# One copy moved behind three others in the experts' loop, and a sum put ahead of a maximum in the attention

## What is computed

```python
def block(args):  # differential attention, per block of 128 queries
    s = jnp.einsum('bhcqd,bhcsd->bhcqs', q_blk, kt).astype(f32) * scale
    p = jax.nn.softmax(jnp.where(mask, s, -jnp.inf), axis=-1)
    attn = p[:, :, 0] - lam * p[:, :, 1]
    return jnp.einsum('bhqs,bhsd->bhqd', attn.astype(v.dtype), vt)

def expert_block(args):  # one expert, on the tokens that chose it
    xb, e = args
    hid = jax.nn.silu(xb @ w_gate[e]) * (xb @ w_up[e])
    return hid @ w_down[e]
```

## Time and profile before

| what | value |
|---|---|
| median of 3 runs | 1429.94 us (1427.81 to 1430.13) |
| the profiled execution, its time | 1428.23 us |
| its span, first to last instruction | 1426.5 us |
| TensorE matmuls busy | 1378.9 us, 97% |
| weight loads busy | 1081.4 us, 76% |
| VectorE busy | 997.4 us, 70% |
| ScalarE busy | 793.3 us, 56% |
| mean granted clock of TensorE | 0.986 |
| the experts | about 350 to 865 us |
| the differential attention | about 122 to 215 us |

### The profile page before, as it was taken

How to read it: one execution, slowest core, us unless ns; L and a number is a source line. 1 busy time by engine, 2 the same in 40 slices (tenths; PEclk the granted TensorE clock), 3 DMA queues, 4 the chain that set the end, 5 groups by cost and what they waited for, 6 DMA issues and landing times.

```text
span 1426.5 us, 20296 instructions
## 1 busy us (share of the span) xinstructions
PE 1378.9 (97%) x6801; PEld 1081.4 (76%) x6802; DVE 997.4 (70%) x1209; ACT 793.3 (56%) x984; POOL 197.5 (14%) x234
## 2 busy tenths in 40 slices
PE   6999999998999999999999989999999999999998
PEld 6887778785777777777777767766888888888886
DVE  7866465657999999999989888675845314343185
ACT  5444457225899999999889882543234212332121
POOL 2021002001232222222222120061000000000000
PEclk8999999999999999999999999999999999999999
DMA  9111115156999999999999976002313313224221
GB/s 353 62 60 59 59 35 177 75 186 265 400 413 408 413 413 413 413 412 412 402 405 410 405 260 255 29 32 92 116 59 119 114 64 118 92 86 162 71 107 59
DMA packets 60967, 302.57 MB, mean 212 GB/s; under 512 B 9700, under 2 KB 11810, under 8 KB 48108
## 3 DMA queue, kind: packets, MB, share of 16 engines
q1 hardware_dynamic: 49420, 282.15, 50.3%
q10 hardware_dynamic: 6288, 11.44, 2.4%
q0 software_dynamic: 5200, 8.18, 1.7%
HBM read 291.74 MB, written 18.87 MB: 218 GB/s over the span
## 4 chain that ended last, share of the span: by engine, by line
PE 74%; DMA 4%; DVE 4%; issue 2%; ACT 2%; POOL 0%; DVEq 0%; SPq 0%; ACTq 0%; POOLq 0%
PE ps L784 14%; PE ps L1066 12%; PE ps L1051 11%; PE ps L823 7%; PE ps L816 4%; PE ps L632 3%; PE ps L793 3%; PE ps L1100 3%; PE ps L884 3%; DMA ring<-in_w_gate 3%; PE ps L956 2%; PE ps L544 2%; PE ps L495 1%; DMA ring<-in_w_in 1%; PE ps L773 1%
## 5 line engine op out<-in xcount | busy, mean ns | idle before, releaser
L2245 DVE TENSOR_TENSOR ring_r<-ring,hi 128x2048 fp32r<-128x2048 f32 (+1 forms) x224 | 431.4, 1980 | 20.3 <-ACT hi L1631 18.9
L1631 ACT ACTIVATE hi<-ring 128x2048 fp32r<-128x2048 f32 (+1 forms) x224 | 362.7, 1661 | 8.5 <-DMA ring<-in_w_gate 7.2
L2259 DVE TENSOR_TENSOR ring_r<-ring,ring_two 128x2048 fp32r<-128x2048 f32 (+1 forms) x50 | 103.8, 2107 | 112.2 <-ACT ring_two L1649 112.2
L1649 ACT ACTIVATE ring_two<-ring 128x2048 fp32r<-128x2048 f32 (+1 forms) x46 | 84.0, 1868 | 132.4 <-PE ps L1066 121.5
L784 PE MATMUL ps<-ring_r,XTS 128*128 128x512 f32 x512 | 129.2, 395 | 5.1 <-DVE ring_r L2245 3.1
L1273 POOL TENSOR_TENSOR rsv<-msv,half 128x1 f32<-128x1 f32 (+2 forms) x32 | 33.0, 1035 | 686.1 <-DVE msv L1818 671.4
L784 PE MATMUL ps<-hi,XTS 128*128 128x512 f32 x512 | 127.4, 391 | 0.0
L1066 PE MATMUL ps<-ring_two,ats 128*128 128x512 f32 x512 | 126.5, 389 | 0.0
L823 PE MATMUL ps<-hi,HIDS 128*64 128x512 f32 x512 | 123.5, 393 | 0.0
L784 PEld LDWEIGHTS ps<-ring_r,XTS 128*128 128x128 f32 x512 | 97.3, 190 | 28.1 <-issue 5.6
L544 PE MATMUL ps<-ring_r,ring_r 128*128 128x512 f32 x448 | 116.4, 409 | 1.0 <-ACT ring_r L1426 0.7
(11 more groups left out here) (366 smaller groups left out, 2219.8 us busy)
## 6 DMA issues: line engine op xcount, KB each, us to landing
ring<-in_w_gate SPq DMA_DIRECT2D x32, 2048.0 KB, 15.8
ring<-in_w_down SPq DMA_DIRECT2D x32, 2048.0 KB, 16.0
ring<-in_w_up SPq DMA_DIRECT2D x32, 2048.0 KB, 17.5
ring<-in_w_ff SPq DMA_DIRECT2D x16, 2048.0 KB, 7.9
ring<-in_w_in SPq DMA_DIRECT2D x9, 2048.0 KB, 9.2
ring<-in_w_out SPq DMA_DIRECT2D x4, 2048.0 KB, 10.6
results<-M SPq DMA_DIRECT2D x4, 1024.0 KB, 16.6
ring<-results SPq DMA_DIRECT2D x8, 512.0 KB, 7.6
```

Source lines behind the costliest of these rows:

```text
L1631: act.activation(HI[u][:, c], ring[:, s, c], ACT.Copy).then_inc(w_hi, 1)
L1649: act.activation(hi_of(u, a, part_size(u)), raw_of(u, a, part_size(u)), ACT.Copy).then_inc(w2_hi, 1)
L2245: vec.tensor_tensor(ring_r[s][:, c], ring[:, s, c], HI[u][:, c].bitcast(F32), ALU.subtract).then_inc(w_lo, 1)
L2259: ins = vec.tensor_tensor(raw_of(u, a, n, ring_r), raw_of(u, a, n), hi_of(u, a, n).bitcast(F32), ALU.subtract)
```

## The change

Three edits. On VectorE, `mixed(n - 1)` moves from behind the maximum, `final_d` and `mean_final` to the head of step n. On ScalarE, the keys of block 3 are copied at step 7, no longer at step 5 (those of block 2 stay at step 3). In the experts, high part 1 of the next gate unit moves from between the silu (L1667) and the gated rows' high parts (L1674) to behind these and the next rows' high part (L1635). Nothing is added or removed, and the count of each semaphore stays.

```diff
@@ scalar, the attention's steps
-                if n in (3, 5):
-                    keys_again(TT - 2 + n // 2 - 1)
+                if n in (3, 7):
+                    keys_again(TT - 2 + n // 4)
@@ scalar, block_act
                 act.activation(SG, ps[:, 2, 0:FT * BLK].rearrange("p (f b) -> p f b", f=FT),
                                ACT.Silu).then_inc(sg_ready, 1)
-                if ahead:
-                    weights_hi(e + 1, 1, 1 - odd)
                 for pair in range(2):
                     act.wait_ge(hid_gated, g * 2 + (pair + 1))
...
                 rows_hi(g + 1)
                 if ahead:
-                    for part in range(2, 5):
+                    for part in range(1, 5):
                         weights_hi(e + 1, part, 1 - odd)
@@ vector, the attention's steps
             for n in range(len(ITEMS) + 2):
+                if 1 <= n <= N_D:
+                    mixed(n - 1)
                 if n < N_D:
                     maximum(n)
...
-                if 1 <= n <= N_D:
-                    mixed(n - 1)
```

## The result

| what | before | after |
|---|---|---|
| median (lowest to highest of 5 runs) | 1429.94 us (1427.81 to 1430.76) | 1439.0 us (1434.23 to 1444.45) |
| ratio to before, 95% interval | | 1.0075, 1.0053 to 1.0097 |
| the profiled execution: time, span | 1428.23, 1426.5 us | 1439.0, 1437.3 us |
| TensorE matmuls busy | 1378.9 us, 97% | 1382.1 us, 96% |
| mean granted clock of TensorE | 0.986 | 0.984 |

The kernel is slower by 0.75% by the ratio of the runs; the two medians differ by 9.1 us, 0.63%. H is still the start of the gated rows' high parts; its line is L1672 in the changed kernel, and the other lines behind the edits moved by one or two as well. The experts lose 15.0 us, the attention gives 6.7 back.

A forecast was written before the change was run, and what follows sets the result against it. The prediction took a loop through ScalarE's copies and VectorE's low parts, 15.56 us per expert, to set the pace. Profiled 1428.2 + 13 (experts) + 8 (clock) - 5 (mixer) = 1444 us, range 1434 to 1454.

The forecast's parts named there:

- The loop: Experts, through ScalarE's copies and VectorE's low parts: copy 1 adds 0.97, 0.24 returns, period 15.56 to 16.29 us; stage +13.
- Idle time before H: Experts, ScalarE: a sign of being right was about 0.8 us idle before the gated rows' high parts.
- TensorE's wait at L816: Experts: TensorE would wait 0.19 + 0.73 = 0.92 us for the gated rows' high part in each expert.
- The clock: Experts: longer TensorE waits let its clock drop, 0 to 30 times at about 0.8 us; 10 drops taken, 8 us.
- Rival C: Experts: the clock falls in nearly every expert, 24 us instead of 8, total 1460; chance 0.10.
- The stream: Experts' weights: no longer binds at period 16.29; gate units land in 9 to 12 us to the end.
- rival B: Experts: the weights' stream sets the stage's end, so 4 to 5 of the 13 us remain, total 1427; chance 0.06.
- The last two periods: End of the experts: the period after expert 29 is set by TensorE and stays; the last is 0.7 us longer.
- The attention: Mixer: the sum ahead of the maximum removes 3.2 us of TensorE waits and a 1.7 us clock loss; -5, bounds 0 and -7.
- Rival D: Mixer: no gain because another wait takes over; total 1449, with few drops 1441; chance 0.10.
- The keys' move: Attention, key copies going from step 5 to 7: nothing either way, 0.5 us at most.
- Rival A: Experts: ScalarE's 1.16 us idle absorbs the copy, period stays 15.56, only the mixer's 5 us show, total 1423; chance 0.08.

The follow-up runs named there:

- the third place: Kernel before with only high part 1 of the next gate unit moved, to ahead of the up result's copy: 1427.9 us, period 15.56.
- the kernel with copy 5 first: High part 5 copied ahead of the two result copies: in the changed kernel 1433.99 us, period 16.06; in the kernel with the attention's edits alone 1426.14 us, period 15.86.
- the filled wait: Changed kernel plus matmuls with unused results ahead of TensorE's wait for the gated rows' high part: seven took 1454.83 us, three 1436.0 us.
- the lighter stream: Only half of each down unit loaded, one run each: on the kernel before 1413.59 us, on the changed kernel 1433.95 us.
- the swap alone: Kernel before with only VectorE's sum (`mixed`) moved ahead of the maximum, keys still copied at step 5: 1425.78 us, one run.

## Why the prediction was right, point by point

The forecast was 1444 (1434 to 1454), slower at 0.87; 1439.0 was measured. The mechanism of the experts' part is the one forecast. That the total is 5 us off and not more is partly luck: the stage lost 6 us less than forecast and the attention gained 1.7 more, while 2.4 us that the forecast left at nothing came in elsewhere.

- **The loop.** Forecast 16.29, measured 16.22. Its pieces, in the order of the forecast: 0.89, 5.50 for four copies (forecast 0.97 + 4.56), 0.95 for the result copies, 1.96, 6.61, 0.31. So the loop from row to row was the right one; 0.07 off, 2 us over the stage. Copy 1's old place was worth nothing, as said, and the third place shows that an empty place costs nothing. That low parts 3 and 4 "end just before copy 5 does" holds within 0.17 us; VectorE's side of the loop is as long as 16.06, as the kernel with copy 5 first shows.
- **Idle time before H.** Forecast 0.8, measured 1.56. From the silu to H it was 608.69 to 609.96, 1.27 us, filled by silu and copy 1; now it is 619.34 to 621.28, 1.94, that is 0.67 more, and only the silu's 0.39 is in it. The forecast counted the growth and left out the place of the copy itself. This time is not on the path.
- **TensorE's wait at L816**: 0.92 forecast, 0.87 measured.
- **The clock.** Forecast 10 falls at 0.8, 8 us; measured 6 at 0.92, 5.5 us (three in the experts' edit alone, with the same wait). The number of falls was the mis-sized term. The count could be bounded only, and the price was right. Rival C gave a fall in nearly every expert. The Trainium skill, "TensorE: Matmul & The Clock Gate", section "A second HAM failure mode: psum-queue depth-cycling", has frequent tiny pauses make the clock swing between its levels; the mechanism is borne out by the filled wait, in one expert of five.
- **The stream.** Landing times of 9.6 to the end, as said; rival B took nothing from the loop. But the price of the move holds only against a kernel that lost 8.4 us to the stream; the lighter stream shows 25 us. In the forecast's working 10.4 us in 18 experts is 0.58 each and not 0.54, which changes nothing.
- **The last two periods.** Forecast +0.7; measured 35.3 instead of 36.6 us, -1.3. The wrong step was to treat the exit from the loop as fixed. The experts' edit alone has 20.53 for the first of them, as before, against 18.02 here. What goes with it is the clock. In the eight of the thirteen kernels in which the clock falls in it this period is 19.97 to 21.90 us, in the five others 16.22 to 18.02. TensorE's pause at the exit, 3.55 before and 3.04 here, is 1.70 to 4.26 us in the other kernels and is gone in the two with TensorE's wait filled. Why it differs stays open. This period in the kernel before, then in the changed one:

```profile
820.68:841.21 20.53, 17.15 (x80) 12.60 (x79) 15.23 (x12) 14.45 (x16) 3.11 (x4) 0.92 0.97 365
834.82:852.84 18.02, 15.36 (x78) 11.32 (x76) 15.21 (x11) 14.47 (x16) 3.44 (x4) 1.00 0.98 355
```

- **The stage's sum.** 13 + 8 = 21 forecast, 15.0 measured: 2.0 of the difference is the period, 2.5 the falls, 2.0 the last periods (0.3 of the forecast lay ahead of the first H).
- **The attention.** Forecast -5 with bounds 0 and -7; measured -6.7 in the stage. The waits for the sum are 3.7 us less (4.7 to 1.0) and both falls of the clock are gone, 3.4 at the forecast's price of 1.7; of these 7.1 us 6.7 are seen. The forecast had 3.2 and one fall. The fall near 138 us isn't tied to the edit, since it stands at 136 in the run with the attention's edits alone. Rival D is refuted.
- **The keys' move.** "Nothing, 0.5 at most" was wrong alone (1.3 us of the wait, 2.8 of the stage) and right beside the swap.
- **Not foreseen**: +1.8 at the start and +2.8 ahead of the first H, with 3.4 us more at the lower clock in each. Kernels with the same edit of the attention show them or not, so they aren't tied to that edit; whether they belong to the single execution or to the kernel, one profile of each can't tell. One profiled span carries some 5 us of this, beside a difference of 10.8 between the spans.
- **Rival A**, the period stays, is refuted by 16.22. The rule tied to it, in the Trainium skill, "Perfetto Trace Analysis", section "Identifying the Most-Contended Engine", looks at the busiest engine first. For TensorE it goes, beside the share of the peak rate, by the weight loads' share, which is 75% here (222.62 of 295.00 us), so that VectorE, at 96%, would be first and ScalarE, at 92%, second and not third. That an engine further down can be rearranged freely isn't said there; it was the prediction's own step, and 16.22 refutes it. ScalarE has 1.56 us idle before each H now, and yet its order helps to set the pace.

Shown by runs are thus the place of copy 1 (three places of it) and the cause of the falls in the loops (the filled wait, in one profiled execution each of two kernels). Left open is why the attention's 6 us are seen as 2 to 3 in the whole kernel, and what decides in which expert the clock falls.

The attention's edits alone, with copy 1 in its old place, take 1425.97 us, 0.15% below the kernel before; the kernel with copy 5 first (1426.14) and the one run of the swap alone (1425.78) can't be told from it.

## What to carry to other kernels

Where several engines are nearly full, write the loop down from start to start across the engines and ask of each moved instruction whether it stands on it. Idle time of the engine told nothing here, neither that a place was free nor that leaving it would gain. Before a copy is moved into a "free" slot, look at what it overwrites, since the wait for the last reader may be as long as what stood there. And a gain of a few us in one stage has to be read from that stage, as the rest of two profiled spans differed by as much here.

## What was unexpected in the hardware

- A wait of only 0.87 us in each period of 16.22 us made the granted clock fall from 1.00 to 0.50 for 3.4 us in every fifth expert, six times in a row, each time some 0.3 to 0.9 us behind H; with 0.81 of the wait filled it fell in none. In the experts' edit alone, with the same waits, it fell in three experts only. With waits of 0.5 in each period of 15.86 us it fell in none, with 0.7 in each of 16.06 in four.
- An f32 matmul of 128x64 values stands in the records as two. Three in a row took 599.04 - 598.23 = 0.81 us, 0.27 each; seven took 0.23 each.
- TensorE at 475.94 busy of 476 us gave a shorter stage, 503.5 us, than TensorE at 457.94 of 476, 511.2 us, with the same useful work.
